# Low parts of the weights by an adding transfer, and a fourth channel tile of the convolution on VectorE

## What is computed

```python
def mixer_conformer_conv(x, w_pw1, b_pw1, w_dw, b_dw, ln_g, ln_b, w_pw2):
    h = x @ w_pw1 + b_pw1
    a, g = jnp.split(h, 2, axis=-1)
    h = a * jax.nn.sigmoid(g)
    h = causal_depthwise_conv(h, w_dw) + b_dw
    h = jax.nn.silu(layer_norm(h, ln_g, ln_b))
    return h @ w_pw2
...
    for i in range(DEPTH):
        ...
        x = layer_norm(ALPHA * x + h, ln1_g[i], ln1_b[i])
        x = layer_norm(ALPHA * x + swiglu(x, ffn_w_gate[i], ffn_w_up[i], ffn_w_down[i]), ln2_g[i], ln2_b[i])
        gate = jax.nn.sigmoid(x @ ple_w_gate[i])
        x = x + gate * rms_norm(p[i] @ ple_w_proj[i], ple_norm_g[i])
```

## Time and profile before

| | |
|---|---|
| time, three executions | 2602.53, 2602.82, 2604.18 us; median 2602.82 us |
| profiled execution: span from first to last instruction | 2597.9 us |
| median time less that span | 4.9 us |
| TensorE busy | 2574.2 us, 99% of the span |
| VectorE busy | 1421.1 us, 55% |
| ScalarE busy | 1049.3 us, 40% |
| GpSimd busy | 1.4 us |
| mean share of the 16 DMA engines on SyncE's queue | 28.8% |

### The profile page before, as it was taken

How to read it: one execution, slowest core, us unless ns; L and a number is a source line. 1 busy time by engine, 2 the same in 40 slices (tenths; PEclk the granted TensorE clock), 3 DMA queues, 4 the chain that set the end, 5 groups by cost and what they waited for, 6 DMA issues and landing times.

```text
span 2597.9 us, 34084 instructions
## 1 busy us (share of the span) xinstructions
PE 2574.2 (99%) x14649; PEld 2235.0 (86%) x14649; DVE 1421.1 (55%) x1639; ACT 1049.3 (40%) x1692; POOL 1.4 (0%) x10
## 2 busy tenths in 40 slices
PE   9999999999999999999999999999999999999999
PEld 7999888889888898888898898888898999888888
DVE  7978333277454663333784473333677977333276
ACT  6765222226233252222362253222356765222235
POOL 0000000000000000000000000000000000000000
PEclk9999999999999999999999999999999999999999
DMA  5203333324222223333232323333322113333322
GB/s 161 66 26 98 97 97 97 99 88 130 89 98 89 82 90 97 97 98 106 82 98 97 98 74 110 95 97 104 97 90 97 60 36 94 98 96 97 99 84 79
DMA packets 193290, 239.63 MB, mean 92 GB/s; under 512 B 14908, under 2 KB 139124, under 8 KB 193012
## 3 DMA queue, kind: packets, MB, share of 16 engines
q1 hardware_dynamic: 192564, 236.94, 28.8%
q10 hardware_dynamic: 576, 0.52, 0.1%
HBM read 233.21 MB, written 2.10 MB: 91 GB/s over the span
## 4 chain that ended last, share of the span: by engine, by line
PE 91%; DVE 7%; ACT 1%; issue 0%; DMA 0%; SPq 0%; DVEq 0%
PE psum L782 16%; PE psum L781 16%; PE psum L783 16%; PE psum L926 13%; PE psum L799 6%; PE psum L801 6%; PE psum L800 6%; PE psum L840 3%; PE psum L771 2%; PE psum L772 2%; PE psum L777 2%; DVE w_lo L1587 1%; DVE xf L1817 1%; DVE xf L1837 1%; DVE rstd L1829 1%; PE psum L1103 1%
## 5 line engine op out<-in xcount | busy, mean ns | idle before, releaser
L1587 DVE TENSOR_TENSOR w_lo<-raw,w_hi 128x1024 fp32r<-128x1024 f32 x431 | 517.9, 1222 | 566.2 <-ACT w_hi L1175 565.2
L1175 ACT CAST w_hi<-raw 128x1024 fp32r<-128x1024 f32 x431 | 445.1, 1048 | 673.2 <-DMA raw<-in_ffn_w_up_dram 331.8
L781 PE MATMUL psum<-a_hi,w_lo 128*128 128x512 f32 x928 | 361.4, 389 | 0.0
L783 PE MATMUL psum<-a_hi,w_hi 128*128 128x512 f32 x928 | 361.2, 389 | 0.0
L782 PE MATMUL psum<-a_lo,w_hi 128*128 128x512 f32 x896 | 348.8, 389 | 0.0
L781 PE MATMUL psum<-h_hi,w_lo 128*128 128x512 f32 x872 | 341.6, 392 | 0.0
L783 PE MATMUL psum<-h_hi,w_hi 128*128 128x512 f32 x872 | 339.6, 389 | 0.0
L782 PE MATMUL psum<-h_lo,w_hi 128*128 128x512 f32 x856 | 333.4, 389 | 0.0
L926 PE MATMUL psum<-a_hi,w_lo 128*128 128x256 f32 x1088 | 280.1, 286 | 6.7 <-DVE w_lo L1587 5.1
L926 PE MATMUL psum<-a_hi,w_hi 128*128 128x256 f32 x1088 | 276.6, 283 | 0.0
L926 PEld LDWEIGHTS psum<-a_hi,w_lo 128*128 128x128 f32 x1088 | 208.7, 192 | 8.7 <-DVE w_lo L1587 4.6
(11 more groups left out here) (299 smaller groups left out, 4053.9 us busy)
## 6 DMA issues: line engine op xcount, KB each, us to landing
raw<-in_ffn_w_gate_dram SPq DMA_DIRECT2D x176, 256.0 KB, 2.8
raw<-in_ffn_w_up_dram SPq DMA_DIRECT2D x176, 256.0 KB, 3.1
raw<-in_ffn_w_down_dram SPq DMA_DIRECT2D x176, 256.0 KB, 2.8
raw<-in_a_w_pw_dram SPq DMA_DIRECT2D x94, 256.0 KB, 2.9
raw<-in_ple_w_gate_dram SPq DMA_DIRECT2D x64, 256.0 KB, 2.7
raw<-in_b_w_in_dram SPq DMA_DIRECT2D x64, 256.0 KB, 2.9
raw<-in_c_w_in_dram SPq DMA_DIRECT2D x48, 256.0 KB, 2.9
raw<-in_b_w_out_dram SPq DMA_DIRECT2D x32, 256.0 KB, 2.7
```

The costliest lines, as they stand in the source:

```text
L781: pe.matmul(bank(grp.g, j), st_lo, mv_hi, start=(k == 0), stop=False, skip_group_check=by_tiles(grp))
L783: done = pe.matmul(bank(grp.g, j), st_hi, mv_hi, start=False, stop=(ku == last and a == UK - 1), skip_group_check=by_tiles(grp))
L1175: act.copy(hi_u[u % RING], raw_u[u % RING]).then_inc(hi_ready, 1)
L1587: dve.tensor_tensor(lo_u[u % RING], raw_u[u % RING], hi_u[u % RING].bitcast(F32), ALU.subtract)\
```

## The change

Two things are changed together.

**Weights.** For units 6 to 431 (`summed`) the high part is loaded straight into `w_hi` by a transfer that GpSimd issues and that casts to float32r (`load_hi`). ScalarE writes the negated high part into `w_lo` (an activation with scale -1). GpSimd then issues a second transfer of the same weights that adds them into `w_lo` (`add_raw`). TensorE waits for that transfer's landing (`lo_landed`) instead of VectorE. VectorE's `weight_lo` stays for units 0 to 5 alone. On GpSimd's queue the adding transfer of unit u-2 stands ahead of the load of unit u (`ADD_LAG`), and at the third unit of group 1 behind a norm both outstanding ones do. Units of one matrix take one transfer of 512 KB each way, units of two matrices (`conv_in`, `short_in`, `ffn_in`) two of 256 KB each way.

**Convolution.** `PHASED` is now tiles 4, 5 and 6. VectorE makes all taps of tiles 2 and 3 together. Shared blocks, `convolve_alone` and `phase_add` go; `centre` stands at step 24 of the third phased tile; `save_centre` stands earlier among ScalarE's diagonals.

```diff
-K_SHARED = 6
-SHARED = 2
-PHASED = ((4, 0), (5, 0), (3, K_SHARED), (6, 0))
+PHASED = (4, 5, 6)
+ADD_LAG = 2
...
         def lo_of_unit(u):
-            return lo_ready, u + 1
+            if u in summed:
+                return lo_landed[u % RING], sum_landings(u)
+            return lo_ready, lo_counts[u]
...
+        summed = range(RING, totals["unit"])
...
+            if grp.unit + k0 // UK in summed:
+                return [((whole, whole), view[:, rows, starts[0]:starts[0] + BANK])]
             return [((whole, i), view[:, k0 + i, starts[0]:starts[0] + BANK]) for i in range(UK)]
...
-                        load(u, parts_of(s, grp, ku * UK))
+                        if u not in summed:
+                            load(u, parts_of(s, grp, ku * UK))
...
+            def load_hi(u):
+
+                s, grp, ku = unit_place(u)
+                pool.wait_ge(*slot_freed(u))
+                dst = hi_u[u % RING].rearrange("p (a n) -> p a n", a=UK)
+                for to, view in parts_of(s, grp, ku * UK):
+                    pool.dma_start(dst[to], view).then_inc(hi_landed[u % RING], 16)
+
+            def add_raw(u):
+
+                s, grp, ku = unit_place(u)
+                pool.wait_ge(hi_ready, u + 1)
+                dst = lo_u[u % RING].rearrange("p (a n) -> p a n", a=UK)
+                for to, view in parts_of(s, grp, ku * UK):
+                    pool.dma_start(dst[to], view, accum_op=ALU.add).then_inc(lo_landed[u % RING], 16)
+
+            added = summed[0]
+            for u in summed:
+                s, grp, ku = unit_place(u)
+                after_norm = s.kind in ("ffn_in", "ple_gate") or s.kind == "mixer_out" and s.layer % 3 == 0
+                held = after_norm and grp.index == 1 and ku == AHEAD
+                while added < (u if held else u - ADD_LAG + 1):
+                    add_raw(added)
+                    added += 1
+                load_hi(u)
+            while added <= summed[-1]:
+                add_raw(added)
+                added += 1
...
             def split(u):
-                act.wait_ge(raw_landed[u % RING], 32 * (u // RING + 1))
-                act.copy(hi_u[u % RING], raw_u[u % RING]).then_inc(hi_ready, 1)
+                r = u % RING
+                if u in summed:
+                    act.wait_ge(hi_landed[r], sum_landings(u))
+                    act.activation(lo_u[r], hi_u[r].bitcast(F32), ACT.Copy, scale=-1.0).then_inc(hi_ready, 1)
+                    return
...
                 for u in range(lo_end[0], min(end, totals["unit"])):
-                    weight_lo(u)
+                    if u not in summed:
+                        weight_lo(u)
...
                         for t in (h_hi, h_lo):
                             for z in range(2):
                                 no_block(t, z * (TAPS_A + 1) * TILE_ROWS)
-                            last = no_block(t, SHARED_AT + (TAPS_A - K_SHARED + 1) * TILE_ROWS)
-                        last.then_inc(no_blocks, 1)
-                        more_blocks(s, 3, 0, phase_part(3))
+                        more_blocks(s, 2, 0, PHASE_PART)
                         act.wait_ge(prod_ready, s.prod0 + 4)
+                        conv_hi(s, 2)
                         conv_hi(s, 3)
-                        conv_hi(s, 4)
...
                         phase_place(s, 1)
+                        save_centre(s)
+                        for part in range(2, PARTS_TO_EVICT):
+                            last_diags(s, part)
                         phase_evict(s, 2)
...
                         gated_input(s, s.groups[3])
                         conv_lo(s, 2)
-                        for part in range(2):
-                            make_shared_blocks(s, part)
-                        convolve(s, 2, *w, 4, K_SHARED, TAPS_A, "a_b_dw", fresh=False, lo_end_at=ahead)
                         conv_lo(s, 3)
-                        conv_lo(s, 4)
+                        convolve(s, 2, *w, 4, TAPS_A, TAPS_A, "a_b_dw", fresh=False, lo_end_at=ahead)
                         lo_to(ahead)
                         lo_more(AHEAD)
-                        convolve_alone(s, 2, K_SHARED, TAPS_A)
-                        phase_add(s, 2)
                         norm_centre_sum(y)
```

118 lines of the change are left out of this document (48 added, 70 removed).

## The result

The changed kernel takes 2712.94 us (median of four, 2708.32 to 2717.26) against 2602.68 us before (four, 2600.62 to 2604.18): a ratio of 1.0426, 95% interval 1.0411 to 1.0441. It is 110 us slower. The prediction had the direction, and the time lies in its range, but it forecast 35 us: the cost is three times what was worked out.

The account below looks back on a forecast made before the run. TensorE, busy 99% of the span, was taken to bound the kernel. The median of 2602.8 us plus 14.2 for the convolution stages and 20.8 for the weights' way gave 2638 us; 8-in-10 range 2608 to 2790.

Parts of the forecast that it names:

- Part 1: Convolution stages: TensorE sheds 156 matmuls, 9.4 us a layer, 18.8 us in both, worthwhile only if what follows is ready earlier.
- Part 2: Convolution stages: VectorE's extra taps make `ysum` ready at 147.95, 16 us after TensorE; 7.1 us a layer longer, +14.2 us.
- part 3: The weights' way: free in the steady state, waits for adding transfers behind norms; +20.8 us in all.
- the stall of the first near unit in `conv_mixer`: Third unit of group 1 behind a convolution's norm: low part lands 2.05 us late, +4.1 us for two.
- The issuing rival: GpSimd's four issues a unit become the bound from 1.36 us each; at 1.5 us 122 us more, 2760 us; chance 0.2.
- The rival in time at `centre`: Both convolution stages: `ysum` ready by 131.9, so the stage gives 18.8 us instead of costing 14.2; 2605 us; chance 0.04.
- the one of cancelling parts: Whole kernel: the change's two parts cancel or do nothing that can be measured; chance 0.04.
- The six norms, and units 28 and 29: Second unit of group 1: 2.45 us at six norms, +14.7; 1.0 us in `ffn_in` at two others, +2.0.
- A: Time from ScalarE's step to the landed low part, replacing VectorE's 1.22 us: taken as 5.7 us, between 4.6 and 6.5.
- In the steady state it costs nothing: Weights away from norms: a slot is freed 27 us before its unit is needed, so both transfers fit; no cost.
- The rival of the full DMA engines: All units: adding transfers fill the DMA engines; at 2.5 loads each +277 us, 2915 us; chance 0.1.
- k: Cost of an adding transfer in loads: DMA share 0.32 (1 + k), full from 2.1, 0.96 at 2.

Follow-up runs that it names:

- w_no_load: weights_alone with the first transfer of each unit left out, so only the adding transfer follows ScalarE's step (result differs); 2635.20 us, ratio 1.0130.
- conv_alone: The changed kernel with the convolution's change only, all weights made the old way; 2628.02 us against 2602.33 before, ratio 1.0098.
- w_no_load_plain: w_no_load with the second transfer writing the weights over the low part instead of adding (result differs); 2610.59 us, ratio 1.0035.
- far_k15: Kernel before, with adding transfers for 271 units in eight long stretches and K_SHARED 15 in place of 6; 2596.51 us against 2601.03, ratio 0.9982.
- w_lag3: weights_alone with ADD_LAG 3: a load stands behind the adding transfer three units back, not two; 2705.51 us, ratio 1.0396.
- w_lag_mixed: weights_alone with lag 3 for loads ahead of norms and lag 2 behind norms; 2657.19 us, ratio 1.0219.
- w_plain: weights_alone with a plain second transfer that overwrites the negated high part instead of adding (result differs); 2623.04 us, ratio 1.0082.
- weights_alone: The kernel before with the weights' half of the change only, convolution as before; 2691.74 us against 2602.46, ratio 1.0353.

## Why the prediction was right or wrong

**Right.** The direction. Part 1: TensorE sheds 156 matmuls a layer and gains nothing by it. Part 2: `ysum` at 148.1 by the prediction's clock against 147.95, the wait at `centre` 16.3 us against 16; ScalarE's cast ended at 108.9 by that clock, where the prediction had 108.9. In part 3: the stall of the first near unit in `conv_mixer`, 2.05 us by the prediction, is 1.9 and 2.1 in w_no_load, where the adding transfer is alone. The issuing rival was rightly a rival and is out: two issues follow each other at 0.73 us (511.76 is one; 525.14 to 525.87 the distance), half of its 1.36, and GpSimd is busy 47%. The rival in time at `centre` and the one of cancelling parts are out.

**Wrong, first: the stage's length was short by its clock.** The prediction let everything behind `centre` follow "as before", 7.1 us a layer with a bound of 8.5. Measured were 9.7 and 12.7 (22.4 in place of 14.2). In layer 0 `centre` came 7.1 us later, where the prediction had 6.8, and 2.6 us more were lost behind it, where it had 0.3. 1.8 of them, and 1.0 in layer 3, are TensorE's slow clock behind the wait: from `centre` to the next unit the changed kernel takes 26.9 and 26.0 us, the runs that hold the clock 25.1 and 24.9. 3 us in layer 3 are ScalarE standing for weights, which is visible in the timelines and absent in conv_alone, though no run removed that alone.

**Wrong, second, and largest: part 3's sum, +20.8 us, measured 80 to 89.** It failed in three steps, all in what the sum takes to be free.

- *The six norms, and units 28 and 29, as one stalled unit each.* The term had A = 5.7 us and one unit, 2.45 us. A by itself is 6.9 for a unit of two transfers (0.3 to the issue, 6.5 to the landing), over the upper bound of 6.5, and 6.0 to 6.4 for one. And the unit ahead of it, which had 4.57 us from ScalarE's step to TensorE's need, no longer fits either; it delays the sums of the second half, and with them ScalarE's next step, so both stalls count. With the adding transfer alone the norms cost 31.0 us where the terms give 16.7 (14.7 and 2.0); up to 10 of the 31 are slow work, the last step below. w_no_load_plain shows that it is this landing time: a plain transfer leaves 9.9.
- *"In the steady state it costs nothing", taken to hold up to the norm.* It holds in the long stretches (far_k15), but two places that the prediction doesn't name lose 35 us: last groups (18.0) and entries (16.9). In the last groups the new way, 0.3 + 7 + 1.05 + 0.3 + 7 us, needs 16 of the ring's 27 us, so a load that goes out 9 us late behind an adding transfer leaves 2 us. The prediction saw that "a late ScalarE now delays a load too", checked it behind the norms alone, and dismissed it. The ring wins back only some 0.5 us a unit: in the changed kernel unit 30's low part lands 1.7 us ahead of need and unit 50's 12.2 us, 20 units later. This pace is the order's too. The load of a unit goes out right behind the adding transfer of the unit two back, so two units take one load's landing (7.2 us), ScalarE's step (1.1) and the way to and through GpSimd's issues (1.8): from the load of unit 42 (318.9) to that of unit 44 (329.0) 10.1 us, 5.0 a unit. In w_lag3 the loads of units 32 to 36 follow each other at 3.6 us. w_lag3 and w_lag_mixed show that the last groups are the queue's order: 18.0 us became 4.7 and 2.0. w_plain, with the same order, loses nothing there: its transfers land in 4 to 5 us, so both the order and the long landings are needed. At the entries the prediction missed that ScalarE's queue has its steps for the next layer's weights ahead of the sigmoids, so that a late load holds up the activations themselves.
- *Every stall at its own length.* No term had the clock. By the table's last column TensorE was busy 21.8 us longer in weights_alone on the same matmuls, over a fourth of its 80.2 us, most of it in work at the granted clock of 0.50 behind its waits.

**The rival of the full DMA engines is out, but its edge was a warning.** It wanted k over 2.1, an adding transfer at over 2.1 loads, and a loss on every unit. The pages give k = 2.0 against SyncE's load, the value that the prediction called "still under", far_k15 shows no loss on 271 units, and w_lag3's 1.30 shows that the engines had room left. What two such transfers a unit did was to each other's landing: 7 us in place of 4 for the load and 5.8 for the adding transfer alone.

Two of the prediction's bounds don't come out of its terms: 17 and 30 on 2602.8 are 2650, not 2665, and the issuing rival at 1.55 us is 2804, not 2790. Neither bears on the outcome.

What stays open: how the remaining 10 us of w_no_load_plain behind norms divide between slow work (up to 4.6), the 0.3 us on the way over GpSimd and a plain landing that is longer than VectorE's 1.22 us; how much of the 29 us of longer busy time would come back with the clock held; why the medians of w_lag_mixed gain more than its trace; and the 5 us between the parts' sum and the whole.

## What to carry to other kernels

A step moved off a relaxed engine into a transfer trades 1.2 us of work for 6 to 7 us of latency; where the consumer has reserve in tens of microseconds that is free (271 units here), where it has 3 us it is a stall at each unit in turn, so choose by the distance from free slot to need, unit by unit. Before moving work to an engine that shows 55% busy, look where its next consumer waits: the same move paid 7 us when the work moved was cut to what VectorE had just been relieved of (9 taps a layer), and cost 26 us at 26 steps a layer. When a queue issues one unit's second transfer ahead of another unit's first, work out the time round that loop and how much of a delay it can win back per unit, and look at what each engine's queue holds behind its wait for a transfer. And price a stall of TensorE with the slow work behind it, not with its length alone.

## What the runs showed that was not expected

- Per byte, a transfer that casts took 1.2 times the engines' time of SyncE's plain load, and an adding one 2.0 times (32.9, 54.1 and 28.8% of the spans). Alone, an adding transfer of 512 KB lands in 5.7 to 5.9 us (units 22, 97 and 221 in w_no_load), in the changed kernel in 7.2.
- In waits of 16 to 20 us for `ysum` TensorE's granted clock was at 0.50 after 2 to 5 us of idle time, and it stayed there for 4 to 6 us of new work, 1 to 2 us of time. Matmuls that nobody reads held it in layer 0. Behind waits of 2 to 8 us it was at 0.50 as well, some 54 us in all in the changed kernel outside the two convolution stages.
- A matmul of the phased form (64 rows by 256 columns) takes 0.12 us alone and 0.06 us each when it alternates with its partner on the other 64 rows.
